# RMS norms over all channels: the root and the reciprocal on one column per 128 tokens instead of on 128 equal rows

## The reference

```python
def rms_norm(x, g):
    xf = x.astype(jnp.float32)
    y = xf * lax.rsqrt(jnp.mean(xf * xf, axis=-1, keepdims=True) + NORM_EPS)
    return (y * g.astype(jnp.float32)).astype(x.dtype)
```

## Time and profile before

| what | value |
| --- | --- |
| three runs | 2338.53, 2340.09, 2341.24 us (median 2340.09) |
| profiled execution | 2340.37 us, its span 2338.5 us |
| mean granted clock | 0.96 |
| TensorE busy | 2179.5 us, 93% |
| VectorE busy | 976.9 us, 42% |
| ScalarE busy | 704.1 us, 30% |

### The profile page before, as it was taken

One profiled execution on the slowest core, in us unless ns is written; L12 is line 12 of the kernel. 1 busy time (PEld: TensorE's weight loads), 2 busy tenths in 40 slices (PEclk: granted clock), 3 DMA queues, 4 the chain that ended last, 5 costly groups with the idle time before them and its releaser, 6 DMA issues.

```text
span 2338.5 us, 22954 instructions
## 1 busy us (share of the span) xinstructions
PE 2179.5 (93%) x9389; PEld 1378.6 (59%) x9389; DVE 976.9 (42%) x1536; ACT 704.1 (30%) x1155; POOL 14.0 (1%) x28
## 2 busy tenths in 40 slices
PE   5999969999999999996989999989999779999997
PEld 2644444333333347554458887866976437888785
DVE  1126240111111144478366665335346327666534
ACT  4136221110111031265233333232124534333322
POOL 1000000000000000000000000000000000000000
PEclk8999979999999999997999999999989799999998
DMA  9316517999999952200113322221220012332210
GB/s 310 127 54 227 188 72 287 409 409 409 409 409 407 406 189 76 70 5 1 54 55 96 103 91 90 90 90 55 91 72 1 0 36 72 91 90 90 96 49 36
DMA packets 199995, 345.67 MB, mean 148 GB/s; under 512 B 14955, under 2 KB 137435, under 8 KB 196691
## 3 DMA queue, kind: packets, MB, share of 16 engines
q1 hardware_dynamic: 198272, 342.02, 41.0%
q0 software_dynamic: 944, 1.91, 0.3%
q10 hardware_dynamic: 675, 0.27, 0.0%
HBM read 342.06 MB, written 2.11 MB: 147 GB/s over the span
## 4 chain that ended last, share of the span: by engine, by line
PE 89%; DVE 7%; ACT 3%; issue 1%; DMA 1%; ACTq 0%; DVEq 0%
PE bank L1499 20%; PE bank L952 17%; PE bank L1513 11%; PE bank L1381 10%; PE bank L1397 5%; PE bank L1361 3%; PE bank L643 3%; PE bank L815 3%; PE bank L622 3%; PE bank L1407 3%; PE bank L633 2%; PE bank L893 1%; PE bank L1302 1%; DVE work L704 1%; PE bank L968 1%; DVE small L711 1%
## 5 line engine op out<-in xcount | busy, mean ns | idle before, releaser
L1499 PE MATMUL bank<-h_high,ring_low 128*128 128x512 f32 x672 | 267.0, 397 | 0.0
L422 ACT ACTIVATE w_high<-ring 128x2048 fp32r<-128x2048 f32 x86 | 163.5, 1904 | 343.6 <-PE bank L1499 201.1
L1499 PE MATMUL bank<-low_ff,w_high 128*128 128x512 f32 x672 | 265.4, 395 | 0.0
L1499 PE MATMUL bank<-h_high,w_high 128*128 128x512 f32 x672 | 263.7, 392 | 0.0
L429 DVE TENSOR_TENSOR ring_low<-ring,w_high 128x2048 fp32r<-128x2048 f32 x86 | 196.2, 2283 | 112.7 <-ACT w_high L422 112.6
L1513 PE MATMUL bank<-ff_split,w_high 128*128 128x512 f32 x704 | 221.2, 395 | 1.6 <-DVE work L1958 1.6
L1873 DVE SCALAR_TENSOR_TENSOR xT<-bank,mod,xT 128x512 f32<-128x512 f32 x64 | 48.1, 751 | 295.3 <-PE bank L1407 294.6
L952 PE MATMUL bank<-hT,ring 128*128 128x512 f32 x352 | 156.3, 598 | 3.1 <-DVE hT L795 2.4
L1513 PEld LDWEIGHTS bank<-ff_split,w_high 128*128 128x128 f32 x704 | 132.6, 188 | 33.3 <-DVE work L1958 2.4
L1499 PEld LDWEIGHTS bank<-h_high,w_high 128*128 128x128 f32 x672 | 126.1, 188 | 32.2
L1499 PEld LDWEIGHTS bank<-h_high,ring_low 128*128 128x128 f32 x672 | 126.1, 188 | 31.2
(11 more groups left out here) (256 smaller groups left out, 3216.9 us busy)
## 6 DMA issues: line engine op xcount, KB each, us to landing
ring<-in_ffn_w_up SPq DMA_DIRECT2D x88, 512.0 KB, 4.9
ring<-in_w_down SPq DMA_DIRECT2D x32, 1024.0 KB, 12.5
ring<-in_w_up SPq DMA_DIRECT2D x30, 1024.0 KB, 11.5
ring<-in_w_gate SPq DMA_DIRECT2D x27, 1024.0 KB, 11.6
ring<-in_w_ada SPq DMA_DIRECT2D x24, 1024.0 KB, 4.9
ring<-in_ffn_w_down SPq DMA_DIRECT2D x22, 1024.0 KB, 4.8
work<-in_w_gate SPq DMA_DIRECT2D x16, 1024.0 KB, 11.3
work<-in_w_down SPq DMA_DIRECT2D x16, 1024.0 KB, 12.1
```

The source lines that it names most:

```text
L422: act.activation(w_high[:, n % 2, 0:words], slab_view(g)[:, 0:words], ACT.Copy).then_inc(sem("split_high"), 1)
L1499: mm = pe.matmul(bank[n % 6][:, :], st[k], mv[k], start=(k == 0), stop=(k == len(st) - 1))
```

## The change

The sums of squares are computed as columns. The activations' squares become the weights and one column of ones moves, so that each 128 tokens have their sum on 128 partitions, one column for each of four groups of tokens: four matmuls of one column for each tile k instead of one of 512 columns. Root and reciprocal then work on 128x4. To have the factor on all partitions along the tokens again, `wide_spread` runs four matmuls of 128 columns (the inverse column, broadcast, as weights, and the identity as what moves) into a PSUM bank. The in-chain norms scale from that bank directly; for the late norms ScalarE copies it to `root`, and VectorE waits for the copy. `inverse_col` is now what the reciprocal writes, so `turn_inverse_pe` is gone. `root_table` runs a root of one column ahead of the squares, which loads ScalarE's table there. The down projection's banks are squared and copied in another order, so that bank 7 is free for the spread.

```diff
-        DOWN_ORDER = [6, 0, 1, 2, 3, 4, 5, 7]
+        DOWN_ORDER = [6, 7, 0, 1, 2, 3, 4, 5]
...
+        def root_table(act):
+            act.wait_ge(sem("eps_set"), 1)
+            act.activation(idle_col, eps_col, ACT.Sqrt)
...
         def wide_root(act, name):
-            act.activation(root[:, :], bank[6][:, :], ACT.Sqrt, scale=1.0 / D, bias=eps_col)\
+            act.activation(sqrt_col, bank[6][:, 0:TT], ACT.Sqrt, scale=1.0 / D, bias=eps_col)\
                .then_inc(sem("norm_root"), 1)
...
         def wide_sum(pe, name, k):
             pe.wait_ge(sem("norm_squared"), s0 + k + 1)
-            pe.matmul(bank[6][:, :], ones, square[:, k % SQ, :], start=(k == 0), stop=(k == DT - 1))\
-              .then_inc(sem("norm_summed"), 1)
+            for i in range(TT):
+                mm = pe.matmul(bank[6][:, i:i + 1], square[:, k % SQ, P * i:P * i + P], ones[:, 0:1], start=(k == 0 and i == 0),
+                               stop=(k == DT - 1), skip_group_check=True)
+            mm.then_inc(sem("norm_summed"), 1)
...
         def wide_inverse(dve, name):
-            dve.reciprocal(root[:, :], root[:, :]).then_inc(sem("norm_inverse"), 1)
-            dve.wait_ge(sem("norm_inverse"), n0 + 1)
+            dve.reciprocal(inverse_col, sqrt_col).then_inc(sem("norm_inverse"), 1)
...
+        def wide_spread(pe, name):
+            pe.wait_ge(sem("norm_inverse"), BEFORE[name][1] + 1)
+            for i in range(TT):
+                mm = pe.matmul(bank[SPREAD_BANK[name]][:, P * i:P * i + P], inverse_col[:, i:i + 1].to_broadcast([P, P]), ident,
+                               start=True, stop=True)
+            mm.then_inc(sem("root_spread"), 1)
...
         def add_normed_dve(dve, name, src, gain):
             wide_inverse(dve, name)
+            dve.wait_ge(*spread(name))
...
-                    dve.scalar_tensor_tensor(normed[:, k % 2, :], src[:, k, :], gain(k), root[:, :], ALU.mult, ALU.mult)\
+                    dve.scalar_tensor_tensor(normed[:, k % 2, :], src[:, k, :], gain(k), spread_root(name), ALU.mult, ALU.mult)\
                        .then_inc(sem("norm_tile"), 1)
...
         def gain_x_act(act, name, ready, gain):
...
             wide_root(act, name)
+            act.wait_ge(*spread(name))
+            act.activation(root[:, :], spread_root(name), ACT.Copy).then_inc(sem("root_copied"), 1)
```

More of the change, by code:

```diff
@@ L231, in build @@
         inverse_col = small[:, 65:65 + TT]
+        sqrt_col = small[:, 70:70 + TT]
+        idle_col = small[:, 95:96]
         a = Area()
@@ L804, in wide_square @@
             act.activation(square[:, k % SQ, :], x, ACT.Square).then_inc(sem("norm_squared"), 1)
+        SPREAD_BANK = {"mix": 7, "ffn": 5, "evpost": 7, "fpost0": 7, "odpost": 7, "fpost1": 7, "evpre": 7, "fpre0": 7, "odpre": 7,
+                       "fpre1": 7}
+        def root_table(act):
+            act.wait_ge(sem("eps_set"), 1)
+            act.activation(idle_col, eps_col, ACT.Sqrt)
         def wide_root(act, name):
@@ L820, in wide_inverse, with spread, spread_root @@
             dve.wait_ge(sem("norm_root"), n0 + 1)
-            dve.reciprocal(root[:, :], root[:, :]).then_inc(sem("norm_inverse"), 1)
-            dve.wait_ge(sem("norm_inverse"), n0 + 1)
+            dve.reciprocal(inverse_col, sqrt_col).then_inc(sem("norm_inverse"), 1)
+        def spread(name):
+            return sem("root_spread"), WIDE.index(name) + 1
+        def wide_spread(pe, name):
[4 more added lines that the diff above has]
+            mm.then_inc(sem("root_spread"), 1)
+        def spread_root(name):
+            return bank[SPREAD_BANK[name]][:, :]
         def wide_scale(dve, name, gain, inverted=False):
@@ L827, in wide_scale @@
                 wide_inverse(dve, name)
+            dve.wait_ge(*spread(name))
             for k in range(DT):
-                dve.scalar_tensor_tensor(hT[:, k, :], xT[:, k, :], gain(k), root[:, :], ALU.mult, ALU.mult)\
+                dve.scalar_tensor_tensor(hT[:, k, :], xT[:, k, :], gain(k), spread_root(name), ALU.mult, ALU.mult)\
                    .then_inc(sem("norm_scaled"), 1)
@@ L848, in norm_x_act @@
         def norm_x_act(act, name, ready):
+            root_table(act)
             for k in range(DT):
@@ L895, in start_late_pe, with root_there @@
                         mm.then_inc(sem(f"{step}_done"), 1)
[L897 to L906, removed]
+            wide_spread(pe, name)
+        def root_there(name):
+            return sem("root_copied"), LATE.index(name) + 1
         def late_out_dve(dve, step, i, o, m, w, tile=None, scale=1.0):
@@ L960, in project_pe @@
                 wide_sum(pe, norm, len(tiles) - 1)
+                wide_spread(pe, norm)
         def start_pe(pe, banks, tiles, kts, after=None):
@@ L1239, in _ @@
                 mm.then_inc(sem("x_turned"), 1)
-            for k in range(DT):
-                wide_sum(pe, "mix", k)
+            norm_x_pe(pe, "mix")
             pe.wait_ge(sem("silu_c"), 1)
@@ L1516, in ffn_pe @@
                 pe.wait_ge(sem(f"down{i}_copied"), 1)
-                norm_x_pe(pe, f"fpost{i}")
+                for k in range(DT):
+                    wide_sum(pe, f"fpost{i}", k)
+                pe.wait_ge(sem(f"down{i}_copied"), 2)
+                wide_spread(pe, f"fpost{i}")
             ffn_pe(0)
             start_late_pe(pe, "odin", "odpre", odin_tiles[0:2])
-            project_pe(pe, "odin", [0, 1, 2, 3], odin_tiles, skip=2,
-                       after=lambda i: turn_inverse_pe(pe, "odpre") if i == 3 else None)
+            project_pe(pe, "odin", [0, 1, 2, 3], odin_tiles, skip=2)
             pe.wait_ge(sem("odin_copied"), len(odin_tiles))
@@ L1902, in _ @@
             wide_inverse(dve, "evpre")
+            dve.wait_ge(*root_there("evpre"))
             for i, (o, m, w) in enumerate(evin_out):
@@ L1951, in ffn_dve @@
                 wide_inverse(dve, f"fpre{i}")
+                dve.wait_ge(*root_there(f"fpre{i}"))
                 cw = VEC["ffn_conv_w_2"] + 132 * i
@@ L1993, in _ @@
             wide_inverse(dve, "odpre")
+            dve.wait_ge(*root_there("odpre"))
             sq_at = len(odin_out) - TT - 4
             for i, (o, m, w) in enumerate(odin_out):
-                if i == 12:
-                    inverse_columns_dve(dve, link, "odpre")
                 late_out_dve(dve, "odin", i, o, m, w, None if w == S else i % TT,
```

5 lines of the change are left out of this document (1 added, 4 removed).

## The result

The changed kernel takes 2391.19 us (median of 4 runs, 2389.27 to 2395.72). Beside it the kernel before took 2340.59 (4 runs, 2338.53 to 2341.24). The ratio is 1.0222, with a 95% interval of 1.0206 to 1.0237: slower by 50.6 us. The forecast was 2386, range 2345 to 2400.

The account below looks back on a forecast made before the run. TensorE, busy 93% of the span, was taken as the bound. Mix 3.0, ffn 2.4, evpre 8.9, evpost with fpre0 8.7, fpost0 with odpre 12.4, odpost with fpre1 8.6, fpost1 2.4 gave +46.4: 2386 us, range 2345 to 2400.

Parts of the forecast that it names:

- The mechanism: TensorE's clock: one-column matmuls neither hold nor lift it, so narrow sums cost 1.73 us at half clock, 0.86 at full.
- The late norms: fpre0, odpre, fpre1: eight tiles at half clock take 20.6 us against 12.6, matmuls behind start cold: +10.0 us each.
- Evpre: Late norm entered at full clock: clock falls 3 us in, tiles take 17.8 us against 10.9; +8.9 with matmuls behind.
- Mix: First norm: longer sums, spread and slabs, partly hidden by idle time: +3 us, between 0 and 7.5.
- The hoisted table load: ScalarE's root table loaded ahead of the squares: said to lie already under the sums, so costing nothing.
- The cover: At mix, TensorE's idle 4.65 us in a DMA wait was to hide part of 10.5 us of added work.
- the lone sums: Sums of ffn, fpost0 and fpost1: 3.9 us longer as the clock falls, less 1.55 for the chain: +2.4 each.
- Evpost: Chain from its last sum to fpre0: shorter root and reciprocal, less the spread: -2.2 us.
- odpost: Chain from its last sum to fpre1: shorter root and reciprocal, and less of an exposed table load: -2.3 us.
- The first: Rival: TensorE being occupied is what counts, all clocks stay and the kernel gets faster: -11.4, 2329 us; chance 0.12.
- The second: Rival: clocks stay but a narrow record costs 0.12 us instead of 0.108: -5, 2335 to 2338 us; chance 0.06.
- The third: Rival: only pure narrow work goes cold, a third of wide columns keeps the clock: +7.5, 2348 us; chance 0.10.

Follow-up runs that it names:

- e1: Changed kernel with 128 columns of ones moving in each sum instead of one: 2334.06 us, ratio 0.9972 to the kernel before.
- e8: Changed kernel with one more, unread 512-column f32 matmul ahead of each of the 32 late sums: 2393.56 us, ratio 1.0224 to the kernel before.
- e2: Kernel before with the change only in the four late norms (evpre, fpre0, odpre, fpre1): 2382.18 us, ratio 1.0175 to the kernel before.
- e4: Changed kernel with 32 columns moving in each sum instead of one: 2383.08 us, ratio 1.0183 to the kernel before.
- e3: Kernel before with the change only in evpost and odpost: 2340.22 us, ratio 0.9999 to the kernel before.
- e5: Kernel before with the change, at 128 moving columns, only in ffn, evpost, fpost0, odpost and fpost1: 2333.7 us, ratio 0.9969 to the kernel before.
- e7: Changed kernel with 128 moving columns in the four late norms only, one in the other six: 2356.78 us, ratio 1.0067 to the kernel before.
- e9: e5 plus unread 512-column matmuls filling TensorE's gaps behind evpost, fpost0 and odpost: 2323.5 us, ratio 0.9924 to the kernel before.
- e11: e9 plus two unread 512-column matmuls between ffn's spread and the router: 2322.92 us, ratio 0.9927 to the kernel before.

## Why the prediction was right, point by point

**The mechanism held.** The prediction said that one-column matmuls neither hold nor lift the clock. It took this from the router and the output's transposes, and no row of the kernel before could show the mixture itself. The trace after shows it directly (0.50 for 15 us of full occupation), and e1 and e8 show that it is the cause, and not only there beside it: more columns or more work on the same records bring the clock and the time back.

**The late norms.** Predicted 2.58 us per tile and 20.6 us for eight, measured 2.56 and 20.63. The parts were a little off in opposite directions: a narrow sum takes 1.50 us at half clock and not 1.73, but the two wide matmuls with their weight loads 1.06 and not 0.85. Behind them L924 takes 9.77 us, +2.4 against the +2.0 predicted. For fpre0, odpre and fpre1 together 31.8 us were predicted and 31.8 measured.

**Evpre was oversized.** The clock was taken to fall 3 us into the tiles. It fell 7 us in:

```profile
870.00:871.00 1.00, 1.00 (x10) 1.00 (x9) 1.00 (x3) 0.89 (x3) 0.00 (x0) 0.92 0.00 0
871.00:872.00 1.00, 1.00 (x5) 0.81 (x4) 1.00 (x2) 0.98 (x2) 0.00 (x0) 0.50 0.00 0
```

Five tiles then ran at 1.36 us and three at 2.42 to 2.56; +5.0 instead of +8.9. The 3 us were worked out from idle gaps. They aren't simply too short, though. In e2 the same loop, entered at full clock too, lost it after 3.9 us:

```profile
859.00:860.00 1.00, 1.00 (x7) 1.00 (x8) 1.00 (x3) 0.69 (x2) 0.00 (x0) 0.66 0.00 0
```

and took 17.25 us, close to the 17.8 predicted. When the clock falls in a loop like this varies from trace to trace, so part of the miss at evpre is chance.

**Mix was mis-sized: +8.0 for +3.0,** above the 7.5 that was given as the end of its range. Its chain in the changed kernel (before, the sum starts at 23.48):

```profile
24.24 1.28 ACT L814
...
26.31 13.83 PE bank L827 x64
...
40.77 2.08 PE bank L843 x8
42.85 2.86 PE bank L1275 x16
...
45.73 6.46 DMA ring<-in_w_ada
```

Three things are there. The hoisted table load (L814), which the prediction said lay under other work, lies on the path here and delays the squares; the kernels that hoist it start mix's sums at 25.4 to 26.3 us, those that don't at 23.5 to 24.7, so it is 1 to 2 us. The sum is at half clock from its first record: 13.83 us, 6.7 more. And the slabs start at 42.85 instead of 30.61, while the wait for a slab behind them shrinks only from 10.74 to 6.46 us: the ring is refilled as TensorE counts its slabs off, so a late first slab makes the transfers behind it late. The cover was taken to be 4.65 us of idle time and was used up. So the table load was put at nothing and cost 1 to 2 us, and the late refill of the ring was named for the range but left out of the 3.0.

**The chains and the lone sums.** Evpost -1.5 for -2.2 (root 0.28 instead of 0.20, the spread 2.09 at half clock), odpost -2.4 for -2.3. For odpost that is luck in part: the row counts from the last sum, and ahead of it the hoisted table load put 1.28 us and the 0.20 us root behind it on the chain (1933.81), which the prediction had under the sums. From the slab split to fpre1's first matmul the changed kernel gains 0.65 us (36.39 for 37.04), and shorter attention stretches hide the difference in the table's last row. Ffn +3.0, fpost0 +3.0 and fpost1 +3.8 for +2.4 each: the sums were taken to be 3.9 us longer and are 4.4 to 5.2. Against the forecast, mix adds 5.0, the lone sums 2.6, evpost 0.7 and the stretches elsewhere 0.8, and evpre takes off 3.9: 5 us in all, the distance of the time from it.

**The rivals.** The first (the clock doesn't care, 2329) is refuted by the windows. Its arithmetic for the rest of the change was near: e1, in which the clock is kept up by 128 columns, is at 2334. The 5 us between are the table loads at mix and odpost (1.6 and 1.5), the longer half clock behind the shorter gaps (1.8 over three norms) and the three lone sums (0.8). The second (a narrow record at 0.12 us) falls with the rows: 0.79 us for eight, 0.099 each, at full clock. The third (only lone sums go cold, 2348) is refuted by e2, in which the late norms alone cost 42 us.

**Left open:** why the up projections take 233.0 us in some fed kernels and 235.2 in all others, why the clock holds ahead of odpost in some profiled executions (the changed kernel, e1, e4) and falls there in others (e3, e5, e7, e8, e9, e11), and when it falls in evpre. Each is worth 2 to 4 us, as much as the attention stretches vary from run to run.

## What to carry to other kernels

A matmul that moves few columns per weight load is only as cheap as its records if TensorE's clock is up without it. Before making operands narrower, read the granted clock of the stretch and of the stretch behind it: here 3.6 us saved per norm on root and reciprocal were paid for with 8 us in the next loop. Where a lightly fed loop follows a gap of TensorE, try feeding the gap: kernels with matmuls whose result nobody reads were 10 us faster, twice, of which 4.5 and 5.8 us are seen at the places fed. And 128 ones instead of one as the moving operand were worth 57 us for the same records.

A saving counts only where it was exposed: five of ten norms had theirs hidden, and in the others the next phase handed part of it back. And work that is hoisted out of a chain must have cover where it lands: the table load came back on the chain at mix and at odpost.

## What the runs showed of the hardware that was not expected

- The same loop of the same shapes (e4, 32 columns) held a full clock for 11.03 us and didn't lift a half one in 20.69. Whether it would hold the full clock for good isn't shown.
- A narrow f32 sum (eight records, 128x128 weights, one column) takes 0.79 us at full and 1.50 us at half clock, so its weight loads nearly follow the array's clock. The Trainium skill (TensorE: Matmul & The Clock Gate, LDWEIGHTS) gives 0.107 us for 128 columns without mention of the array's clock; the trace has 0.099 and 0.188 us per record.
- Work that nobody reads was almost free where it brought the clock back: 27.5 us of it, as costed at full clock, for 2.4 us (e8).
- The same idle time did not always cost the clock: ahead of odpost TensorE stood idle for 2.7 us in e1 and in e3, and the granted clock stayed at 1.00 in e1 and was at 0.50 in e3 when TensorE restarted.
- Mix's old sum took 7.13 us in some profiled executions and 10.14 to 10.18 in others (e3, e5): the clock at the start of the program isn't the same each time. Here it cost nothing, since the wait for a slab behind the sum shrank by as much.
